# High and low weight words side by side in one buffer, read by TensorE with a step of two words

## The chip, the cores and the metric

The kernel runs on one core of a Trainium2 chip, in one launch. The metric is the device time of that core in microseconds (us). The engines are named as in the profile: PE is TensorE's matmul, PEld its weight load, DVE is VectorE, ACT ScalarE, POOL GpSimd and SP SyncE, which issues the transfers.

## The reference

Two layers of one block and then two layers of another, on 512 tokens of width 1024. Cut to the matrix products that matter here:

```python
# first block, twice
h = x @ w_in[l]                                  # 1024 -> 10k columns
proj   = einsum('bsnc,ncd->bsnd', branches, w_o_branch[l])
merged = sum(sigmoid(merge + b_gate) * proj, axis=2)
x      = layer_norm(alpha * x + merged @ w_out[l])
# second block, twice; in its first layer the 256 context tokens go through too
zx, zc = hx @ w_in[i], hc @ w_in[i]
x, ctx = x + ga1 * (mx @ w_out[i]), ctx + cga1 * (mc @ w_out[i])
x   = x   + ga2 * swiglu(fx, w_gate_up[i], w_down[i])
ctx = ctx + cga2 * swiglu(fc, w_gate_up[i], w_down[i])
```

Everything is float32. A recurrence (RWKV), two attentions, a convolution and a Fourier mix stand between these products; their own matrix products do not use the buffers that are changed.

## The kernel before

**Weights as a stream of chunks.** All weights are laid out in HBM as 414 chunks of 128 partitions by 1024 words; a chunk is eight 128x128 tiles side by side. The class `Stream` (from L92) takes them through a ring of three buffers (`send`, L112). Most chunks, 376 of them, are used at more than one pass of precision: such a chunk is split into a high part of type float32r and a low part, the remainder. ACT makes the high part by a copy with conversion (`hi`, L123), POOL the low part by a subtraction (`lo`, L131). There are two slots for highs and two for lows (`PARTS = 2`). `hi` of a chunk may start when the split chunk two before it has been left by PE, which PE says with a semaphore on the first matmul of the next chunk; `lo` waits for `hi`, and a new transfer into the ring waits for `lo`.

**Products from three passes.** Activations too are held as a high and a low tensor of float32r. For each 128x128 tile of weights PE runs three matmuls: high weights by high activations (L155 or L163), high weights by low activations (L158 or L166), low weights by high activations (L723, L1717, L2140, L2369, L167 and others). In `three` the three passes stand directly one after another for each tile; in the other form the two passes with high weights run over the whole chunk first, and the passes with low weights follow, so that they have more time to be made. The weights are the stationary operand, and PE loads them anew for every matmul, a load of 128 columns. The moving operand is the activation: 512 tokens, or the 256 context tokens in the first layer of the second block.

**What sets the order.** Each stage is a block in which every engine has its own instruction list, written out by hand, with semaphores between them; the lists of PE, ACT and POOL call `stream.hi`, `stream.lo` and the matmul helpers at fixed places. In the last stages of layer 1 (output projection and the two down projections, class `Project`) a chunk is used by `three` and by 512 columns only, and its low part has to be there when its first tile begins.

**One other reader.** Before the feed forward of each layer, and at the opening of the last layer, PE runs ten matmuls on a high part alone, as both operands, while it waits for the norm (L2205). Nothing reads what they write.

The functions below name the parts only as `stream.high(n)` and `stream.low(n)`, which come from the two fields `highs` and `lows` of `Stream`.

Of the kernel before, what the change touches and what calls it, by code (L numbers as in the profile page):

```python
# [17 lines left out]
F32R = mybir.dt.float32r  # L18
# [4 lines left out]
P = 128  # L23
# [17 lines left out]
RING = 3  # L41
PARTS = 2
CW = 1024
# [131 lines left out]
def build(nc, A):  # L175
    with ExitStack() as ctx:
        def sb(name, shape, dt=F32):
            return ctx.enter_context(nc.sbuf_tensor(name, shape, dt))

        pools = [[nc.alloc_semaphore(f"stage{p}_{i}") for i in range(47)] for p in range(3)]  # L180
        arrived = [nc.alloc_semaphore(f"chunk_arrived{i}") for i in range(RING)]
        used = nc.alloc_semaphore("chunks_used")
        hi_made, lo_made = nc.alloc_semaphore("high_made"), nc.alloc_semaphore("low_made")
        loaded = nc.alloc_semaphore("loaded")
        stored = nc.alloc_semaphore("stored")
        constants = nc.alloc_semaphore("second_constants")
        PS = ctx.enter_context(nc.psum_tensor("ps", [P, 8, 512], F32))
        turn = [0]

        def stage():  # L190

            turn[0] += 1
            return Names(pools[turn[0] % 3]), pools[(turn[0] + 1) % 3]

        WR = (sb("ring", [P, RING, CW]), sb("highs", [P, PARTS, CW], F32R), sb("lows", [P, PARTS, CW], F32R),
              arrived, used, hi_made, lo_made)
        mods = sb("mods", [P, LAYERS, 96])

        XH, XL = sb("x_high", [P, DK, T], F32R)[:, :, :], sb("x_low", [P, DK, T], F32R)[:, :, :]
        BR = sb("BR", [P, NB * WT, T])  # L200

        def weights(n):
            if n < SECOND:
                return A["w1"][n // NCHUNK1, n % NCHUNK1, :, :]
            return A["w2"][n - SECOND, :, :]

        split = [NCHUNK1 * layer + n for layer in range(LAYERS) for n in SPLIT1] + SPLIT2
        stream = Stream(WR, weights, split)
        with ExitStack() as one:
            merged = first(nc, one, A, PS, XH, XL, BR, stream, mods, stage, loaded)  # L210
        with ExitStack() as two:
            second(nc, two, A, PS, XH, XL, BR, stream, mods, stage, constants, stored, merged)
# [2888 lines left out]
```

## Time and profile before

| | us |
|---|---|
| median of 2 runs | 3352.69 (3351.68 to 3353.70) |
| the profiled execution | 3352.91 |
| its span in the trace | 3351.1 |
| PE busy in the span | 3206.5 (96%) |
| PEld busy | 2516.6 (75%) |
| POOL, DVE, ACT busy | 1485.4, 1508.9, 1183.9 |
| mean granted TensorE clock | 0.989 of full speed |

The profiled execution is 0.2 us above the median and its span 1.8 us shorter than its time. "Busy" is time in which at least one instruction of the engine is in flight, so that matmuls and loads which overlap are not counted twice in a total, while the mean duration of one is longer than the pace at which they follow one another.

### The profile page before, as it was taken

To read this page: it belongs to the slowest core of one execution; us is meant where nothing else is said; L and a number is where in the kernel's file an instruction comes from. 1 tells how busy PE (TensorE), PEld (TensorE's weight loads), DVE (VectorE), ACT (ScalarE), POOL (GpSimd) and SP (SyncE) were. 2 spreads that over 40 slices of the span, in tenths; PEclk is the share of its full clock that TensorE was granted. 3 is DMA by queue.
4 is the path that set the end of the run, shared out by engine and by line. 5 is a ranking of instruction groups with operands and counts; after the bars stand their busy time and mean duration, and the time that the engine had idled before them with its cause. 6 is when DMAs were issued, how large, how long until landed. Compare 5 with 4: busy or idle time off the path is not lost. (4 is left out here: it accounts for less than half of the span.)

```text
span 3351.1 us, 51795 instructions
## 1 busy us (share of the span) xinstructions
PE 3206.5 (96%) x21120; PEld 2516.6 (75%) x21120; DVE 1508.9 (45%) x2374; ACT 1183.9 (35%) x1940; POOL 1485.4 (44%) x820
## 2 busy tenths in 40 slices
PE   8899999999999999999998989999999998999999
PEld 6784786888668747868876756788888875678787
DVE  7633374999575333949996235300100022520000
ACT  6224433422353434252225445322122243532221
POOL 4421553444353235545442276344234434745454
PEclk9999999999999999999999999999999999999999
DMA  3011132555220111235543200121122211023232
GB/s 130 8 34 57 57 101 76 208 201 191 78 63 4 46 63 64 94 114 196 206 151 109 66 26 27 51 64 63 57 70 63 63 61 51 16 80 101 92 97 94
DMA packets 77611, 284.18 MB, mean 85 GB/s; under 512 B 8736, under 2 KB 8736, under 8 KB 76864
## 3 DMA queue, kind: packets, MB, share of 16 engines
q1 hardware_dynamic: 77376, 280.88, 25.2%
q8 instruction: 168, 2.75, 0.3%
q14 instruction: 67, 0.55, 0.1%
HBM read 278.75 MB, written 2.10 MB: 84 GB/s over the span
## 5 line engine op out<-in xcount | busy, mean ns | idle before, releaser
L131 POOL TENSOR_TENSOR lows<-ring,highs 128x1024 fp32r<-128x1024 f32 x376 | 941.4, 2505 | 1542.5 <-ACT highs L123 1508.3
L155 PE MATMUL ps<-x_high,highs 128*128 128x512 f32 x2080 | 831.5, 400 | 33.7 <-ACT highs L123 14.9
L158 PE MATMUL ps<-x_low,highs 128*128 128x512 f32 x2080 | 814.3, 391 | 0.0
L123 ACT ACTIVATE highs<-ring 128x1024 fp32r<-128x1024 f32 x376 | 397.0, 1056 | 714.6 <-PE ps L155 375.8
L155 PEld LDWEIGHTS ps<-x_high,highs 128*128 128x128 f32 x2080 | 392.4, 189 | 133.6 <-issue 37.8
L158 PEld LDWEIGHTS ps<-x_low,highs 128*128 128x128 f32 x2080 | 392.8, 189 | 83.8 <-issue 4.8
L1790 DVE CUSTOM_DVE_ANT_0 BR<-BR 128x1024 f32<-128x1024 f32 x144 | 289.4, 2010 | 6.8
L2830 DVE TENSOR_TENSOR hidden_scratch<-ps,hidden_scratch 128x512 f32<-128x512 f32 x44 | 30.4, 691 | 546.5 <-PE ps L2140 538.3
L723 PE MATMUL ps<-x_high,lows 128*128 128x512 f32 x1024 | 252.9, 389 | 0.0
L723 PEld LDWEIGHTS ps<-x_high,lows 128*128 128x128 f32 x1024 | 192.2, 188 | 39.9
L2706 DVE SCALAR_TENSOR_TENSOR BR<-ps,mod,BR 128x512 f32<-128x512 f32 x72 | 47.3, 662 | 364.9 <-PE ps L167 364.9
L163 PE MATMUL ps<-hidden_parts,highs 128*128 128x512 f32 (+1 forms) x528 | 188.0, 356 | 0.0
L167 PE MATMUL ps<-hidden_parts,lows 128*128 128x512 f32 (+1 forms) x528 | 188.0, 356 | 0.0
L166 PE MATMUL ps<-hidden_parts,highs 128*128 128x512 f32 (+1 forms) x528 | 188.0, 356 | 0.0
L471 POOL TENSOR_SCALAR tiles<-tiles 128x768 f32<-128x768 f32 (+1 forms) x80 | 154.8, 1947 | 29.0 <-DVE tiles L498 29.0
L2140 PE MATMUL ps<-x_high,lows 128*128 128x512 f32 x672 | 167.1, 391 | 0.0
L1605 DVE SCALAR_TENSOR_TENSOR ps<-X,par,ps 128x512 f32<-128x512 f32 x232 | 152.9, 741 | 0.0
L2140 PEld LDWEIGHTS ps<-x_high,lows 128*128 128x128 f32 x672 | 123.3, 188 | 24.0
L471 POOL TENSOR_SCALAR X<-X 128x256 f32<-128x256 f32 (+3 forms) x96 | 97.7, 1030 | 67.3 <-DVE X L498 67.2
L492 DVE TENSOR_REDUCE tiles<-ps 128x1 f32<-128x768 f32 (+1 forms) x80 | 67.6, 845 | 109.2 <-PE ps L365 109.0
L166 PEld LDWEIGHTS ps<-hidden_parts,highs 128*128 128x128 f32 x528 | 99.4, 188 | 15.8
L163 PEld LDWEIGHTS ps<-hidden_parts,highs 128*128 128x128 f32 x528 | 99.2, 188 | 16.0
(443 smaller groups left out, 5584.6 us busy)
## 6 DMA issues: line engine op xcount, KB each, us to landing
ring<-in_w SPq DMA_DIRECT2D x414, 512.0 KB, 3.5
BR<-in_ada SPq DMA_DIRECT2D x72, 512.0 KB, 3.5
merging<-in_ada SPq DMA_DIRECT2D x24, 512.0 KB, 3.4
X<-in_xT SPq DMA_DIRECT2D x4, 512.0 KB, 6.5
X<-in_memT SPq DMA_DIRECT2D x2, 1024.0 KB, 5.3
BR<-in_cond SPq DMA_DIRECT2D x4, 512.0 KB, 4.7
out<-BR SPq DMA_DIRECT2D x8, 256.0 KB, 4.5
cst<-in_cst SPq DMA_DIRECT2D x1, 1408.0 KB, 8.0
```

What stands on the lines that cost most here:

```text
L123: nc.scalar.activation(self.high(n), self.chunk(n), ACT.Copy).then_inc(self.hi_made, 1)
L131: nc.gpsimd.tensor_tensor(self.low(n), self.chunk(n), self.high(n).bitcast(F32), ALU.subtract).then_inc(self.lo_made, 1)
L155: mm = nc.tensor.matmul(ps, high, xhigh, start=start, stop=False)
L158: nc.tensor.matmul(ps, high, xlow, start=False, stop=False)
L163: mm = nc.tensor.matmul(ps, high, xhigh, start=start, stop=False)
L166: nc.tensor.matmul(ps, high, xlow, start=False, stop=False)
L167: return nc.tensor.matmul(ps, low, xhigh, start=False, stop=stop)
L471: nc.gpsimd.tensor_scalar(prob(i, u), prob(i, u), stats[:, 3, n:n + 1], None, ALU.mult).then_inc(S("normed"), 1)
L723: mm = nc.tensor.matmul(PS[:, bank, :], tile_of(stream.low(n), k), xh[:, k, :], start=False, stop=(k == DK - 1))
L1605: ins = v.scalar_tensor_tensor(out=ACC[:, c, :] if tap == TAPS - 1 else acc, in0=H0[:, c, tap:tap + T], scalar=w, in1=acc, op0=ALU.mult, o ...
L1790: v.tensor_tensor_reduce(PROD, rows_of(t), CB[:, c, :], 1.0, 0.0, ALU.mult, ALU.add, AD[:, t, c:c + 1]).then_inc(S("ada"), 1)
L2140: mm = nc.tensor.matmul(ps, tile_of(stream.low(n), k), high[:, k, :], start=False, stop=(k == DK - 1))
```

## The change

The two tensors for highs and lows, each of 128 partitions by 2 slots by 1024 words, become one of 128 by 2 by 1024 by 2 words: word 0 of each pair is the high part, word 1 the low part. `highs` and `lows` are now views of it whose neighbouring words lie two words (8 bytes) apart. The size in total, the number of slots, all instructions, their order and all semaphores stay as they are. ACT writes with that step (L123), POOL reads the high part and writes the low part with it (L131), PE loads weights with it, and the matmuls of L2205 read their moving operand with it.

```diff
-        WR = (sb("ring", [P, RING, CW]), sb("highs", [P, PARTS, CW], F32R), sb("lows", [P, PARTS, CW], F32R),
-              arrived, used, hi_made, lo_made)
+        ring, parts = sb("ring", [P, RING, CW]), sb("weight_parts", [P, PARTS, CW, 2], F32R)
+        WR = (ring, parts[:, :, :, 0], parts[:, :, :, 1], arrived, used, hi_made, lo_made)
```

## Rows read from the trace of the kernel before

**Rows 1.** The page: busy time of each engine (share of the span), instructions.
```profile
PE 3206.5 (96%) x21120; PEld 2516.6 (75%) x21120; DVE 1508.9 (45%) x2374; ACT 1183.9 (35%) x1940; POOL 1485.4 (44%) x820
```
**Rows 2.** Busy by stretch, instructions touching highs, then lows (PE, PEld, ACT, POOL).
```profile
0.00:3351.10 3351.10, 1748.99 (x7390) 1320.26 (x7390) 397.00 (x376) 941.43 (x376) 0.99 0.26 85
...
0.00:3351.10 3351.10, 954.76 (x3680) 666.12 (x3680) 941.43 (x376) 0.99 0.26 85
```
**Rows 3.** Groups of PE by shape: out<-moving,weights | busy us, mean ns | idle before.
```profile
L158 PE MATMUL ps<-context_low,highs 128*128 128x256 f32 x416 | 101.9, 283 | 0.0
L155 PE MATMUL ps<-context_high,highs 128*128 128x256 f32 x416 | 101.8, 283 | 0.0
L163 PE MATMUL ps<-hidden_parts,highs 128*128 128x256 f32 x176 | 48.9, 278 | 0.0
L2140 PE MATMUL ps<-context_high,lows 128*128 128x256 f32 x336 | 46.9, 282 | 0.0
L163 PE MATMUL ps<-mixed_parts,highs 128*128 128x256 f32 x64 | 17.7, 277 | 0.0
L2369 PE MATMUL ps<-context_high,lows 128*128 128x256 f32 x80 | 11.2, 282 | 0.0
L163 PE MATMUL ps<-context_high,highs 128*128 128x256 f32 x16 | 4.7, 294 | 0.1
...
L723 PE MATMUL ps<-x_high,lows 128*128 128x512 f32 x1024 | 252.9, 389 | 0.0
```
**Rows 4.** Timeline of PE: start us, us from first start to last end, runs.
```profile
1500.08 2.03 PE L1717 MATMUL ps<-branches_high,lows 128*128 128x512 f32 x8
1505.59 1.98 PE L723 MATMUL ps<-x_high,lows 128*128 128x512 f32 x8
...
2256.24 1.12 PE L2140 MATMUL ps<-context_high,lows 128*128 128x256 f32 x8
```
**Rows 5.** Groups of PEld by shape: weight loads of 128, 96 and 64 columns.
```profile
L158 PEld LDWEIGHTS ps<-x_low,highs 128*128 128x128 f32 x2080 | 392.8, 189 | 83.8 <-issue 4.8
...
L1353 PEld LDWEIGHTS ps<-X,ring 128*96 128x96 f32 x96 | 15.5, 163 | 26.1 <-issue 26.1
...
L392 PEld LDWEIGHTS ps<-tiles 128*64 128x64 f32 x832 | 44.7, 137 | 8.9 <-issue 8.9
```
**Rows 6.** Timeline of PE: float32 by 256 columns, moving step one, then two.
```profile
1803.76 1.46 PE L2322 MATMUL ps<-mixed,ring 128*128 128x256 f32 x6
...
1939.99 1.52 PE L2541 MATMUL ps<-ring,tiles 128*128 128x256 f32 x6
```
**Rows 7.** Lines L2322 and L2541: duration ns min/median/max.
```profile
L2322 PE MATMUL ps<-mixed,ring x64: 378/379/380, 1803.5 to 1835.0; 128*128 128x256 f32 x64
...
L2541 PE MATMUL ps<-ring,tiles x80: 386/592/667, 1939.5 to 2826.3; 128*128 128x512 f32 x64, 128*128 128x256 f32 x16
```
**Rows 8.** Waits: who waited for whom, us in total, times, longest.
```profile
POOL lows L131 <- ACT highs L123: 1508.3, 324, 40.1
...
PE ps L155 <- ACT highs L123: 18.5, 11, 7.2
```
**Rows 9.** Lines L131 and L123: duration ns min/median/max.
```profile
L131 POOL TENSOR_TENSOR lows<-ring,highs x376: 2337/2402/3465, 7.2 to 3338.1; 128x1024 fp32r<-128x1024 f32 x188
...
L123 ACT ACTIVATE highs<-ring x376: 1039/1060/1065, 6.1 to 3337.0; 128x1024 fp32r<-128x1024 f32 x188
```
**Rows 10.** Timeline of POOL and ACT in a down projection of layer 1.
```profile
3133.07 2.39 POOL L131 TENSOR_TENSOR lows<-ring,highs 128x1024 fp32r<-128x1024 f32 x1 [3.20 <-ACT highs L123]
...
3131.93 1.06 ACT L123 ACTIVATE highs<-ring 128x1024 fp32r<-128x1024 f32 x1 [4.54 <-PE ps L163]
3137.53 1.06 ACT L123 ACTIVATE highs<-ring 128x1024 fp32r<-128x1024 f32 x1 [4.54 <-PE ps L163]
```
**Rows 11.** Timeline around the warming matmuls of L2205 in layer 1.
```profile
2977.25 3.77 PE L2205 MATMUL ps<-highs 128*128 128x512 f32 x10 [2.53 <-PEq L2718]
...
2982.33 0.47 PE L163 MATMUL ps<-x_high,highs 128*128 128x512 f32 x1 [1.31 <-DVE x_low L2196]
```
## Prediction

> **What bounds the kernel now.** The page comes first: PE is busy for 96% of the span, twice as long as any other engine, so only what PE does or waits for can move the time [rows 1]. The view of busy time by tile says how much of that the change reaches: 7,390 matmuls take their weights from highs and 3,680 from lows, 11,070 of 21,120, with 1,749 and 955 us of PE time [rows 2]. The groups by shape divide these by the width of the moving operand. The 256-column ones are L158 and L155 with 416 each, L163 of hidden_parts with 176, L2140 with 336, L163 of mixed_parts with 64, L2369 with 80 and L163 of the context with 16; each L163 stands for three lines of equal count, L163, L166 and L167 [rows 3]. That is 416+416+336+80+3x(176+64+16) = 2,016, and leaves 9,054 with 512 columns.
>
> The duration of a matmul is no price, since matmuls overlap; the timeline gives the pace. Eight matmuls of L723 in 1.98 us with 0.389 for the last one are (1.98-0.389)/7 = 227 ns each; eight of L1717 with the same end are 234; eight of L2140 with the context, (1.12-0.282)/7 = 120 ns [rows 3, 4]. The pace follows the moving columns: 256 more cost 107 ns. What does a load take beside that? Loads of 128, 96 and 64 columns last 189, 163 and 137 ns [rows 5], so 52 ns for 64 columns, 0.81 ns a column: 128 columns are about 104 ns of reading and 85 ns of fixed delay, an estimate from the slope. Under a 512-column matmul this read has 227-104 = 123 ns of room, under a 256-column one only 120-104 = 16. The 256-column matmuls are thus where a slower load would show first.
>
> **The change part by part.** No instruction, wait or transfer is added, removed or moved; four kinds of instruction get operands whose words lie two apart.
>
> *Weight loads, 11,070.* The trace of before has no weight load with a step. The nearest row is a moving operand with one: L2541, whose 256-column form takes every second word of the ring. Six of these in 1.52 us, ending with one of about 387 ns (the lowest of this line is 386), are (1.52-0.387)/5 = 227 ns each; L2322, the same float32 by 256 columns with neighbouring words, gives (1.46-0.379)/5 = 216 [rows 6, 7]. Step two costs that stream 5%, at 216/256 = 0.84 ns a word, which is about the rate of a load (0.81). I take this 5% for the load: 104 becomes 110 ns, still under 120, and the cost is nothing; the cover is the streaming of the operand of the matmul before it. If the 6 ns came through all the same, it would be 2,016 x 6 = 12 us; under 512 columns, nothing. Gain is excluded, since the moving operand sets the pace. The other end is a load at half its rate; it is the first rival below.
>
> The Trainium skill, "SBUF — State Buffer", under "Door 1: The DMA port swizzle", says that SBUF has lines of 16 bytes and that an engine keeps full rate as long as it finds two or more of its words in each. Step two leaves exactly two, so by that rule the loads and the reads of L2205 cost nothing at all, and the time would be 3354; the trace's 5% for just this step speaks a little against it. The same page also says that each crossing to a new line pays, and the change doubles the crossings, from 32 to 64 for a load; read in that way it is the first rival.
>
> *L2205, 30 matmuls.* Their moving operand is a high part, 512 words of float32r. L723 streams 512 such words in 227 ns; L2541 needs the same 227 ns for 256 words with step two [rows 4, 6]. I take it that the step halves the rate here: 454 ns, 227 more for each, 2.3 us for the ten of a stage. In the trace they end at 2977.25+3.77 = 2981.02 and PE next waits for x_low of DVE until 2982.33, so 1.31 us are free and 1.0 is left over [rows 11]. There are three such stages: 0 to 3 x 2.3 = 7 us; I take 2.
>
> *ACT's 376 copies.* They last 1,039 to 1,065 ns [rows 9]. Their store now steps by two words, which no ACT row shows. Bounds: nothing, and, as for L2205, twice the time, 1.06 us more. PE waits for a high 11 times, 18.5 us in all [rows 8]; 1.06 on each is 12 us. With the 5% of the nearest stepped row it is 0.05 us on each, 1 us with rounding up. I take 1.
>
> *POOL's 376 subtractions.* They last 2,337 to 3,465 ns, in the middle 2,402 [rows 9], now with one read and the store stepped. POOL waits for ACT 1,508 us in all before them [rows 8], so mostly there is room. The tightest place is where `three` needs the low part at once: the 8+2x11 = 30 chunks of the last projections of layer 1. There ACT starts at 3131.93, when PE's first matmul of the chunk before has ended; the low part is ready at 3133.07+2.39 = 3135.46; and the next start of ACT, at 3137.53, says that PE began the chunk about 0.4 earlier, its load 0.2 before that, at 3136.9 [rows 10]. That is 1.4 us of margin. The nearest row for a slower POOL is its own longest, 3,465, or 1.06 us more: covered. Cost nothing. Should POOL or ACT be faster, nothing comes of it beyond PE's waits for highs, at most 18 us [rows 8].
>
> The Trainium skill, "GPSIMD Engine Reference", "Performance pitfalls for Q7 kernels", makes a read half as dear again once step times element size exceeds 8 bytes. The change stands at 8 exactly; no row here tests it, and by its 50%, 1.2 us, the margin would still hold.
>
> **Sum.** Against the profiled execution's 3352.9: loads 0, L2205 +2, ACT +1, POOL 0, which makes 3355.9. That execution lies 0.2 above the median of the runs, so 3356 it is.
>
> **The rivals.**
>
> *Loads at half their rate (slower).* If a load fetches two words at a time and step two wastes one of them, its read takes 2 x 104 = 208 ns. In the 256-column matmuls it then replaces the stream as what sets the pace: 208, or 208+16 = 224 if the present distance stays, against 120. That is 2,016 x 88 to 104 = 177 to 210 us; under 512 columns 224 still fits in 227. Time 3533 to 3566, say 3550. It decides from a load's read of 120 ns on, and reaches 2% (67 us, 33 ns for each) at 153. For it: the halving that I take myself for L2205. Against it: the load is as slow as the stream of L2541, where the step costs 5% and not 100% [rows 5, 6]. Chance 0.19.
>
> *Loads and streams collide more.* The pace at 512 columns is not one number: 227 for L723, 234 for L1717, with the same shapes and other tensors [rows 4], so something beside the count of columns costs up to 7 ns. If it is the load's read meeting the stream's, twice the stretch of memory may bring those 7 ns everywhere: 9,054 x 7 = 63 us, time 3419. Against it: one path of it would have to reach tensors that show none today. Chance 0.05, half of it beyond 2%.
>
> *The makers of the parts fall behind.* ACT at twice its time and POOL at its longest are 2.12 us more against 1.4 of margin: 30 x 0.7 = 21 us, with the 12 us of the waits for highs 3389. Chance 0.04.
>
> *The parts are made faster.* All of PE's waits for highs gone: 3356-18 = 3338. No row points to it. Chance 0.01.
>
> **How the numbers follow.** My forecast has 0.71: 3356, itself from 3343 (run to run and a few of the waits) to 3375 (12 us for the loads, 7 for L2205). The range must hold 8 in 10; with the makers' 3389 and the collision's 3419 it has 0.71+0.04+0.05 = 0.80, so it ends at 3425 and leaves out the first rival; below, 3340. Two per cent, 67 us, is about what a measurement of this kernel tells from no change. Within it: 0.71+0.04+0.01 and half of 0.05, 0.78. Slower: 0.19+0.02 = 0.21. Faster: 0.01.
>
> **What would show it.** Right: L158 and L2140 with 256 columns keep a busy time near 102 and 47 us; loads from highs last between 189 and 195 ns; L2205 paces near 454 ns; POOL and ACT stay within 1.06 us of now. The first rival: loads from highs and lows near 290 ns, and only the 256-column groups longer. The collision: 512-column matmuls at 234 and more wherever the weights come from the new buffer. The makers: waits of PE for L131 in the last projections. The forecast is wrong if a load's read with step two lasts over 120 ns, for then nothing covers it; and far more wrong if it passes 227, for then all 11,070 matmuls pay.

## The result

The changed kernel takes 3391.64 us (3390.48 to 3392.8, two runs) against 3352.69: a ratio of 1.0112 with a 95% interval of 1.0082 to 1.0141, 39 us more. The number lies in the predicted range and within 2%, but 36 us above the forecast of 3356, so most of what there is to learn lies in that gap. Every sign that the prediction listed for being right (the 256-column groups, loads of 189 to 195 ns, L2205 near 454 ns, POOL and ACT within 1.06 us) came true all the same; none of them looks at the 512-column matmuls. The granted clock was 0.989 in this execution and between 0.983 and 0.992 in the others that are compared here; one of the eleven runs of e5_aligned below took 5353 us at a granted clock of 0.554 and is in no ratio.

First, the page of the changed kernel: busy time of each engine, then the groups that hold most of the weight matmuls (busy us, mean ns | idle before, and what ended it).
```profile
PE 3246.7 (96%) x21120; PEld 2578.2 (76%) x21120; DVE 1517.2 (45%) x2374; ACT 1212.6 (36%) x1940; POOL 1495.2 (44%) x820
...
L155 PE MATMUL ps<-x_high,weight_parts 128*128 128x512 f32 x2080 | 842.1, 405 | 31.9 <-ACT weight_parts L123 13.3
L158 PE MATMUL ps<-x_low,weight_parts 128*128 128x512 f32 x2080 | 824.6, 396 | 0.0
...
L155 PEld LDWEIGHTS ps<-x_high,weight_parts 128*128 128x128 f32 x2080 | 406.2, 195 | 129.3 <-issue 34.6
L158 PEld LDWEIGHTS ps<-x_low,weight_parts 128*128 128x128 f32 x2080 | 405.8, 195 | 83.3 <-issue 4.6
...
L723 PE MATMUL ps<-x_high,weight_parts 128*128 128x512 f32 x1024 | 259.5, 394 | 0.0
```
The same groups of the kernel before, as far as they were not shown yet:
```profile
L155 PE MATMUL ps<-x_high,highs 128*128 128x512 f32 x2080 | 831.5, 400 | 33.7 <-ACT highs L123 14.9
L158 PE MATMUL ps<-x_low,highs 128*128 128x512 f32 x2080 | 814.3, 391 | 0.0
```
PE is as full as before, 96%, and busy 40.2 us longer; it does not wait more (31.9 us of idle time before L155 where there were 33.7). A load of 128 columns lasts 195 ns where it lasted 189 [rows 5]. So the time is not in a wait: the matmuls themselves follow each other more slowly, and it is the wide ones. L723 went from 252.9 [rows 3] to 259.5 us.

The groups by shape of the changed kernel, and the two groups of before that they need beside [rows 3], say which ones.
```profile
L163 PE MATMUL ps<-hidden_parts,weight_parts 128*128 128x512 f32 x352 | 138.5, 393 | 0.0
...
L158 PE MATMUL ps<-context_low,weight_parts 128*128 128x256 f32 x416 | 103.1, 284 | 0.0
...
L1717 PE MATMUL ps<-branches_high,weight_parts 128*128 128x512 f32 x256 | 64.4, 393 | 0.0
...
L163 PE MATMUL ps<-hidden_parts,weight_parts 128*128 128x256 f32 x176 | 49.6, 282 | 0.0
...
L2140 PE MATMUL ps<-context_high,weight_parts 128*128 128x256 f32 x336 | 47.6, 284 | 0.0
```
```profile
L163 PE MATMUL ps<-hidden_parts,highs 128*128 128x512 f32 x352 | 139.1, 395 | 0.0
...
L1717 PE MATMUL ps<-branches_high,lows 128*128 128x512 f32 x256 | 65.0, 395 | 0.0
```
The slow-down is not everywhere. L723 takes 6.6 us more over 1,024 matmuls, L158 of x_low 10.3 more over 2,080. But L1717 (branches) and the wide form of L163 (hidden_parts) are no longer than before, 64.4 for 65.0 and 138.5 for 139.1. The 256-column groups cost a little: 101.9 to 103.1, 46.9 to 47.6, 48.9 to 49.6 us [rows 3].

The timeline of the changed kernel's PE (start us, us from first start to last end) gives the pace, as in [rows 4].
```profile
1519.55 2.01 PE L1717 MATMUL ps<-branches_high,weight_parts 128*128 128x512 f32 x8
...
1525.13 2.03 PE L723 MATMUL ps<-x_high,weight_parts 128*128 128x512 f32 x8
...
2266.33 1.13 PE L2140 MATMUL ps<-context_high,weight_parts 128*128 128x256 f32 x8
```
L723 now paces (2.03-0.394)/7 = 234 ns, where it was 227; L1717 (2.01-0.393)/7 = 231, where it was 234; L2140 with the context (1.13-0.284)/7 = 121, where it was 120. The fast stream has joined the slow ones.

To place all of the difference I summed, over the whole trace, the distances from the start of the matmul before to each matmul's own start; a distance is counted with the later of the two. First to last start is 3340.3 us before and 3377.6 after, 37.3 more. Of these, 26.3 are in the 512-column weight matmuls (32.8 more in distances up to 300 ns, which hold hardly any wait, and 6.5 less in longer ones), 7.7 in the 256-column ones, 4.0 in L2205, and 0.7 less in all the rest. Where both matmuls have the same width and take their weights from the changed buffers, the mean distance up to 260 ns is 227.7 before and 233.1 after with x_high, 228.0 and 233.5 with x_low, 229.2 and 233.1 with merged_high; but 230.7 and 231.8 with branches_high, 237.3 and 231.6 with branches_low, 233.1 and 231.2 with hidden_parts.

### The profile page after: what moved, and what is told of

Same layout as the page of the kernel before. It is cut to its first block and busy times, and to the rows that moved or that the text cites. A ratio compares the mean times of both kernels' runs of the same rounds, so it can differ in the third digit from the quotient of the medians.

```text
span 3388.7 us, 51795 instructions
## 1 busy us (share of the span) xinstructions
PE 3246.7 (96%) x21120; PEld 2578.2 (76%) x21120; DVE 1517.2 (45%) x2374; ACT 1212.6 (36%) x1940; POOL 1495.2 (44%) x820
## 5 line engine op out<-in xcount | busy, mean ns | idle before, releaser
L131 POOL TENSOR_TENSOR weight_parts<-ring,weight_parts 128x1024 fp32r<-128x1024 f32 x376 | 950.9, 2530 | 1571.0 <-ACT weight_parts L123 1535.7
L155 PE MATMUL ps<-x_high,weight_parts 128*128 128x512 f32 x2080 | 842.1, 405 | 31.9 <-ACT weight_parts L123 13.3
L158 PE MATMUL ps<-x_low,weight_parts 128*128 128x512 f32 x2080 | 824.6, 396 | 0.0
L123 ACT ACTIVATE weight_parts<-ring 128x1024 fp32r<-128x1024 f32 x376 | 427.0, 1136 | 720.7 <-PE ps L155 380.0
L155 PEld LDWEIGHTS ps<-x_high,weight_parts 128*128 128x128 f32 x2080 | 406.2, 195 | 129.3 <-issue 34.6
L158 PEld LDWEIGHTS ps<-x_low,weight_parts 128*128 128x128 f32 x2080 | 405.8, 195 | 83.3 <-issue 4.6
L1790 DVE CUSTOM_DVE_ANT_0 BR<-BR 128x1024 f32<-128x1024 f32 x144 | 297.6, 2066 | 6.8
L723 PE MATMUL ps<-x_high,weight_parts 128*128 128x512 f32 x1024 | 259.5, 394 | 0.0
L723 PEld LDWEIGHTS ps<-x_high,weight_parts 128*128 128x128 f32 x1024 | 198.1, 193 | 40.9
L167 PE MATMUL ps<-hidden_parts,weight_parts 128*128 128x512 f32 (+1 forms) x528 | 188.3, 357 | 0.0
L166 PE MATMUL ps<-hidden_parts,weight_parts 128*128 128x512 f32 (+1 forms) x528 | 188.2, 356 | 0.0
L163 PE MATMUL ps<-hidden_parts,weight_parts 128*128 128x512 f32 (+1 forms) x528 | 188.0, 356 | 0.0
L2140 PE MATMUL ps<-x_high,weight_parts 128*128 128x512 f32 x672 | 170.4, 394 | 0.0
L2140 PEld LDWEIGHTS ps<-x_high,weight_parts 128*128 128x128 f32 x672 | 127.0, 194 | 23.4
L163 PEld LDWEIGHTS ps<-hidden_parts,weight_parts 128*128 128x128 f32 x528 | 103.0, 195 | 13.0
L167 PEld LDWEIGHTS ps<-hidden_parts,weight_parts 128*128 128x128 f32 x528 | 103.0, 195 | 12.8
```

Source lines behind the costliest of these rows:

```text
L123: nc.scalar.activation(self.high(n), self.chunk(n), ACT.Copy).then_inc(self.hi_made, 1)
L131: nc.gpsimd.tensor_tensor(self.low(n), self.chunk(n), self.high(n).bitcast(F32), ALU.subtract).then_inc(self.lo_made, 1)
L155: mm = nc.tensor.matmul(ps, high, xhigh, start=start, stop=False)
L158: nc.tensor.matmul(ps, high, xlow, start=False, stop=False)
L163: mm = nc.tensor.matmul(ps, high, xhigh, start=start, stop=False)
L166: nc.tensor.matmul(ps, high, xlow, start=False, stop=False)
```

## Experiments

Each ratio below is against runs of the kernel before on the same chip: 3352.87 us (14 runs) for e1_tiles, e2_highs_step, e3_step4 and e4_gap128, 3351.29 (21 runs) for e2b_lows_step, e5_aligned, e6_step_gap128 and e7_gap64, 3350.88 (15 runs) for e8_second_shift128. **Theory A** is that the step is the cause: a load whose words lie two apart slows the stream that runs beside it. **Theory B** is that the common buffer, or where things lie in memory, is.

### One buffer, unit step

In e1_tiles high and low stand side by side in one buffer of the same size, but tile by tile, so that each load still reads 128 neighbouring words (two lines of the edit; the functions that pick a part and a tile follow it).
```
-  WR = (sb("ring", ...), sb("highs", [P, PARTS, CW], F32R), sb("lows", [P, PARTS, CW], F32R),
+  ring, parts = sb("ring", ...), sb("weight_parts", [P, PARTS, DK, 2, P], F32R)
+  WR = (ring, parts[:, :, :, 0, :], parts[:, :, :, 1, :], ...
```


> High and low parts share one buffer, but in runs of 128 words, one tile of weights each, so that every weight load has neighbouring words and only the blocks alternate. Theory A (the load's own step makes it meet the stream of the moving operand more often): the 512-column matmuls by x go back from 233 to about 227 ns, loads last 188 ns again, ACT's copy 1.06 us, time 3353 +- 8. Theory B (what counts is where the parts lie, not the step): the pace stays near 233 for x, time 3375 to 3392. Theory C (the slower copies of ACT, 72 ns, and POOL, 34 ns, disturb PE): as A, this run does not part A from C.

Measured: 3352.57 us, ratio 1.0 (0.9991 to 1.0009). The page of e1_tiles:
```profile
L158 PE MATMUL ps<-x_high,weight_parts 128*128 128x512 f32 x2080 | 832.0, 400 | 33.9 <-ACT weight_parts L123 15.2
L123 ACT ACTIVATE weight_parts<-ring 128x1024 fp32r<-128x1024 f32 x376 | 397.6, 1058 | 714.9 <-PE ps L158 375.2
```
Its L158 is the L155 of the other kernels, with 832.0 us for 831.5. One buffer for both parts costs nothing, so the first half of Theory B falls; the step remains, and the place.

### Only one of the parts stepped

e2_highs_step steps the high parts alone (over the two slots), e2b_lows_step the low parts alone.
```
e2_highs_step
-  sb("highs", [P, PARTS, CW], F32R)       -  return self.highs[:, self.place[n] % PARTS, :]
+  sb("highs", [P, CW, PARTS], F32R)       +  return self.highs[:, :, self.place[n] % PARTS]
e2b_lows_step: the same two lines for lows
```


> Only the highs are read with step two: the highs of the two slots are interleaved word by word, the lows lie as before, the memory is the same. Theory A: matmuls with high weights by x pace at 233, those of L723 with low weights at 227, loads 195 and 188 ns; about two thirds of the 39 us, time 3375 to 3381. Theory B: no such division by the part; both near one value. Theory C: POOL reads a stepped high as in the change and ACT stores one, so both passes would be slow, L723 at 230 to 233.

> Only the low parts step (by two words, over the two slots); the high parts and both sides of x keep unit step. About a third of the weight loads read the lows, all under 512 columns of x_high and its like. Theory A (each stepped load slows the stream beside it by about 6 ns): L723 and the third passes of x go to 233, the others stay at 227.7: about 3,000 loads by 5.5 to 6 ns, 16 to 18 us, and nothing for the fp32r stream of L2205: 3367 to 3372. Rival (one stepped buffer is enough to spoil the pace of all): 3380 to 3390.

Measured: 3379.61 (1.0083, 1.0068 to 1.0098) and 3363.67 (1.0039, 1.0024 to 1.0055). The page of e2_highs_step:
```profile
L123 ACT ACTIVATE highs<-ring 128x1024 fp32r<-128x1024 f32 x376 | 426.6, 1135 | 722.2 <-PE ps L155 380.6
L155 PEld LDWEIGHTS ps<-x_high,highs 128*128 128x128 f32 x2080 | 405.2, 195 | 130.2 <-issue 36.0
...
L723 PE MATMUL ps<-x_high,lows 128*128 128x512 f32 x1024 | 253.8, 390 | 0.0
L723 PEld LDWEIGHTS ps<-x_high,lows 128*128 128x128 f32 x1024 | 192.3, 188 | 41.4
```
And the page of e2b_lows_step:
```profile
L155 PE MATMUL ps<-x_high,highs 128*128 128x512 f32 x2080 | 830.9, 399 | 32.3 <-ACT highs L123 13.1
...
L155 PEld LDWEIGHTS ps<-x_high,highs 128*128 128x128 f32 x2080 | 392.5, 189 | 130.5 <-issue 35.1
L723 PE MATMUL ps<-x_high,lows 128*128 128x512 f32 x1024 | 259.6, 394 | 0.0
L723 PEld LDWEIGHTS ps<-x_high,lows 128*128 128x128 f32 x1024 | 197.8, 193 | 40.5
```
For the streams of x the cost goes with the stepped load. With stepped highs L155's loads last 195 ns, and L723, which loads the lows, keeps 188 ns and 253.8 us; with stepped lows it is the other way round, 193 ns and 259.6 us. That also answers the third theory of e1_tiles, that the slower copies of ACT disturb PE: ACT's copy lasts 1,135 ns with stepped highs, as in the change, and L723 keeps its time. The two add up: 26.7 and 12.4 us are 39.1, and the whole change costs 39.0. e2b_lows_step missed its range by 3 us from below: of the 3,008 wide matmuls with low weights only 2,144 have x_high and 128 merged_high; 2,272 by 5.5 ns are 12.5 us. The narrow matmuls of hidden_parts do not divide by the part: their mean distance is 114.4 ns before, 119.1 with stepped highs, 119.9 with stepped lows though only a third of their loads step, and 120.1 with both. Why is open.

### Twice the step

e3_step4 lets both slots and both parts alternate word by word, so that each operand steps by four words (against the changed kernel).
```
+  ring, parts = sb("ring", ...), sb("weight_parts", [P, CW, PARTS, 2], F32R)
+  WR = (ring, parts[:, :, :, 0], parts[:, :, :, 1], ...
+  return self.highs[:, :, self.place[n] % PARTS]      (lows alike)
```


> High and low of both slots are interleaved, so that loads, copies and subtractions step by four words, 16 bytes, in the same 16 KB. Theory A (a load reads twice the stretch of memory again): the reads of a load take 4 x the stretch of before; if each 16 bytes costs the load what it costs the moving stream in the trace, 227/128 = 1.77 ns, the load's read is 128 x 1.77 = 227 ns, the 512-column pace 235 to 250 and the 256-column pace about 227 to 240 instead of 120, time 3352 + 9054 x 0.01 to 0.02 + 2016 x 0.11 = 3660 to 3760. Theory B: no slower than the change, 3392. L2205's ten matmuls slow to about 900 ns each, 3 x 4.5 us more, partly seen.

Measured: 3732.78 us, ratio 1.1133 (1.1116 to 1.1149), within the range. The page of e3_step4 and two rows of its PE timeline:
```profile
PE 3538.4 (95%) x21120; PEld 3203.3 (86%) x21120; DVE 1575.2 (42%) x2374; ACT 1560.9 (42%) x1940; POOL 1684.2 (45%) x820
...
L123 ACT ACTIVATE weight_parts<-ring 128x1024 fp32r<-128x1024 f32 x376 | 783.0, 2084 | 768.0 <-PE ps L155 381.9
L155 PE MATMUL ps<-x_high,weight_parts 128*128 128x512 f32 x2080 | 866.0, 416 | 61.5 <-ACT weight_parts L123 41.3
...
L158 PEld LDWEIGHTS ps<-x_low,weight_parts 128*128 128x128 f32 x2080 | 647.4, 311 | 5.9
```
```profile
2481.63 2.16 PE L2140 MATMUL ps<-x_high,weight_parts 128*128 128x512 f32 x8
2483.63 1.92 PE L2140 MATMUL ps<-context_high,weight_parts 128*128 128x256 f32 x8
```
Now the load is slow: 311 ns, 122 more than the 189 of before. Added to the 104 of reading that the prediction estimated, that is 226 ns for one read. In these rows the context paces (1.92-0.397)/7 = 218 ns where it was 120, and x_high (2.16-0.398)/7 = 252 where it was 227. By the sum of distances the 2,016 narrow matmuls take 200.8 us more, 100 ns each. This is the first rival of the prediction, within its price (177 to 210 us), one step further than it was feared: what happens to a load whose read outlasts the stream beside it. It also shows that the change's 6 ns under 512 columns are of another kind, for there the read, 110 ns by the same estimate, leaves half of the stream's 227 unused.

The rest of the range was met partly by luck. The 9,024 wide weight matmuls take 149 us more, but 132 of these lie in distances over 300 ns (500 of them, 254 before), and PE's waits for ACT, 46.1 us against 18.5, are the smaller part of that; the rest is not placed. And L2205, which by the rule of 1.77 ns for each 16 bytes was to slow to about 900 ns, took 464. So the rule fits the load (226 for 227 ns) and not the moving operand, and one fit does not show it.

### The step, or the place

e4_gap128 is the kernel before with 128 bytes put between the weights and everything behind them.
```
+  sb("gap", [P, 32])
   mods = sb("mods", [P, LAYERS, 96])
```


> The kernel before with 128 unused bytes between the lows and what follows, so that x, the branches, the hidden and mixed parts all lie 128 bytes further from the weights (merged parts keep their place). Theory B (the pace of 227 or 233 is set by where operands lie, modulo some hundred bytes): x, now 227, goes to about 233 and costs some 6000 x 6 ns = 36 us, the branches go from 233 to 227; time 3375 to 3390. Theory A alone (only the step counts) has no place for it: paces as before, 3353 +- 8.

e7_gap64 has half the gap, e6_step_gap128 puts the gap of 128 bytes into the changed kernel.

> The kernel before, with 64 bytes instead of 128 between the weights and everything behind them. If the pace goes by the offset within 256 bytes, x comes to the offset (64 behind the weights) from which the hidden values' branch-like 233 can be interpolated: x between 228 and 234, hidden and mixed at the offset opposite the weights. Theory D says a time between 3352 and 3372, by how many streams fall on the slow pace; if the kernel is indifferent to offsets under 128 bytes it stays at 3352 to 3354.

> The changed kernel with 128 bytes between the weights and everything behind them. Theory D1 (a load that steps by two words puts every stream at 233, wherever the operands stand): x stays at 233.1 to 233.5, merged at 233, time 3390 to 3393. D2 (the step only moved x from a good place to a bad one, and another place is good): x at 227 to 229 again, time 3355 to 3365. D3 (step and bad place add): x at 238 or more, time 3410 to 3430.

Measured: e4_gap128 3366.45 (1.0039, 1.0025 to 1.0054), e7_gap64 3355.79 (1.0013, 1.0004 to 1.0022), e6_step_gap128 3380.92 (1.0089, 1.0075 to 1.0102). The page and the groups by shape of e4_gap128 (its lines after L196 are one higher):
```profile
L155 PEld LDWEIGHTS ps<-x_high,highs 128*128 128x128 f32 x2080 | 394.3, 190 | 137.4 <-issue 32.4
...
L724 PE MATMUL ps<-x_high,lows 128*128 128x512 f32 x1024 | 259.3, 395 | 0.0
...
L163 PE MATMUL ps<-hidden_parts,highs 128*128 128x512 f32 x352 | 136.7, 388 | 0.0
...
L1718 PE MATMUL ps<-branches_high,lows 128*128 128x512 f32 x256 | 63.2, 389 | 0.0
```
And the page of e6_step_gap128:
```profile
L155 PE MATMUL ps<-x_high,weight_parts 128*128 128x512 f32 x2080 | 837.0, 402 | 32.7 <-ACT weight_parts L123 14.0
...
L155 PEld LDWEIGHTS ps<-x_high,weight_parts 128*128 128x128 f32 x2080 | 408.1, 196 | 122.5 <-issue 35.6
...
L724 PE MATMUL ps<-x_high,weight_parts 128*128 128x512 f32 x1024 | 257.6, 393 | 0.0
```
For e4_gap128 the paces are those of Theory B, the time is a miss for both: it lies under B's 3375 to 3390 and over A's 3353 +- 8. The wide matmuls take 20 us more in distances up to 300 ns, for B's price was that of x alone and other streams give some back, and 7 us less in all the rest, 4.7 of them in matmuls that the changed buffers do not feed. e7_gap64 came within its range. Its expectation puts hidden and mixed values "opposite the weights", but 64 bytes bring them from 192 bytes past the weights' offset to that offset itself. Without any step, and with loads of the same 190 ns, 128 bytes make L724 (the L723 of before) as slow as the change does, 259.3 us, and make the branches and hidden values faster, 65.0 to 63.2 and 139.1 to 136.7. The mean distances are, with the step in the last two rows:

| kernel | x_high | branches_high, _low | hidden_parts, 512 | time, us |
|---|---|---|---|---|
| before | 227.7 | 230.7, 237.3 | 233.1 | 3352.7 |
| e4_gap128 | 231.9 | 227.3, 227.9 | 228.9 | 3366.5 |
| e7_gap64 | 229.4 | 231.8, 235.1 | 227.7 | 3355.8 |
| changed | 233.1 | 231.8, 231.6 | 231.2 | 3391.6 |
| e6_step_gap128 | 231.6 | 232.8, 232.8 | 233.3 | 3380.9 |

So the pace of a stream at unit step depends on where its operand lies. Counted within 256 bytes from the offset at which every tile of the weights begins, it is 226.7 to 228.0 ns at 0 (x before, branches in e4_gap128, hidden values in e7_gap64), 228.9 to 229.4 at 64 (merged values, hidden in e4_gap128, x in e7_gap64), 230.7 to 237.3 at 128 (branches before, x in e4_gap128) and 231.8 to 235.1 at 192 (hidden before, branches in e7_gap64). The weights themselves were moved in none of these kernels, so whether it is the distance to them that counts, or the operand's own address, is not parted.

With the step none of these streams is below 231 at either place. e6_step_gap128 lies between the theories that it was to tell apart, nearer to the first (every stream on the slow pace) in its paces; against the 3351.3 us of before on its chip it adds 30 us where the change adds 39, and the two intervals overlap. Place has an effect of its own, but it does not explain the change: x begins at the same address before and after it, so does the weights' buffer, and e1_tiles, which moves the tiles about in that buffer, costs nothing.

### Using the place

e5_aligned moves branches, hidden and mixed values to the offset that the weights and x have; e8_second_shift128 moves hidden and mixed values alone, by 128 bytes.
```
e5_aligned                                e8_second_shift128
-  sb("room_edge", [P, 8])                -  spare = sb("spare", [P, 16])
+  sb("room_edge", [P, 40])               +  spare = sb("spare", [P, 48])
-  spare = sb("spare", [P, 16])
+  spare = sb("spare", [P, 32])
```


> Unit step, as before the change, and x and the weights keep their addresses. 128 bytes more stand ahead of the room of the branches and 64 more ahead of the hidden and mixed values, so that both start at the same offset within 256 bytes as the weights, as x does. Theory D (two paces at unit step, set by where the moving operand stands against the weights): the branches' 768 512-column matmuls go from a mean of 232.9 ns to about 227.6 (4.1 us), the hidden values' 1,056 from 233.1 to 228 to 229 (4.3 to 5.4 us), the mixed values' 384 from 233.2 to 228 to 229 (1.6 to 2.0 us), all else unchanged: 10.0 to 11.5 us less, 3341 to 3343. Rival (the paces of 233 belong to those streams for another reason, and the shift by 128 bytes earlier helped them by chance): 3352 to 3353, paces unchanged.

> The kernel before, with 128 bytes more ahead of the hidden and mixed values alone; weights, x, branches and merged values keep their addresses. That puts hidden and mixed 64 bytes past the weights' offset within 256 bytes, where e4_gap128 read 228.9 and 229.4 ns for their 512-column matmuls (233.1 and 233.2 before) and 113.3 ns for the 256-column ones of hidden (114.4 before). No stage fed by the branches changes, so nothing is given to the merging stage, in which VectorE is busy 98% of the time. Placement theory: 1,056 by 4.2 ns, 384 by 3.8 ns and some 700 by about 1 ns are 4.4 + 1.5 + 0.7 = 6.6 us less: a ratio of 0.998. Rival (what PE gains in these stages it waits for later, as with the branches in e5_aligned): the paces fall and the ratio stays within 0.001 of 1.

Measured: 3356.68 us, ratio 1.0014 (1.0005 to 1.0023), and 3350.68 us, ratio 0.9995 (0.9986 to 1.0004). The first is a miss: its paces are those of the theory, and it is 5 us slower than the kernel before, clear of its interval, where the theory had 10 to 11.5 us less and its rival no change. The second has the outcome of its rival, lower paces and a ratio of 1 within 0.001. The groups by shape of e5_aligned:
```profile
L163 PE MATMUL ps<-hidden_parts,highs 128*128 128x512 f32 x352 | 137.5, 391 | 0.0
...
L1717 PE MATMUL ps<-branches_high,lows 128*128 128x512 f32 x256 | 63.2, 389 | 0.0
...
L163 PE MATMUL ps<-hidden_parts,highs 128*128 128x256 f32 x176 | 49.6, 282 | 0.0
```
Its busy time in 40 us of the merging stage (PE, PEld, DVE, ACT, POOL), and PE's waits between 740 and 870 us:
```profile
760.00:800.00 40.00, 36.89 (x162) 29.94 (x161) 39.12 (x45) 12.07 (x15) 18.44 (x7) 1.00 0.60 217
```
```profile
PE ps L155 <- ACT highs L123: 3.1, 2, 1.6
PE ps L155 <- DVE merged_low L1762: 2.1, 1, 2.1
```
The paces fell as foreseen: branches to 226.7 ns, hidden to 227.6, mixed to 227.4. The distances up to 300 ns in the 512-column matmuls sum to 15.1 us less than before. But the longer ones sum to 16.7 us more, and the 256-column ones to 3.2 more: hidden_parts with 256 columns went from 114.4 to 119.5 ns, so the place that is good for the wide form is bad for the narrow one, which I had left out.

Of the longer distances one part can be placed. In the merging stages DVE is busy 39.12 of 40 us, before and now, and PE waits for merged_low from DVE (2.1 us between 740 and 870 us, and 0.2 before). An engine that is full and keeps its pace would take back what PE gained and no more; but between the same matmuls these two stages are 2.3 and 3.6 us longer than before (from 598.6 and 1488.7 us of the trace of before). DVE itself worked longer. Its reductions of L1790, before and in e5_aligned:
```profile
L1790 DVE CUSTOM_DVE_ANT_0 BR<-BR 128x1024 f32<-128x1024 f32 x144 | 289.4, 2010 | 6.8
L1790 DVE CUSTOM_DVE_ANT_0 BR<-merging,BR 128x1024 f32<-128x1024 f32 x48 | 94.1, 1960 | 6.7 <-ACT BR L1751 4.7
```
```profile
L1790 DVE CUSTOM_DVE_ANT_0 BR<-BR 128x1024 f32<-128x1024 f32 x144 | 292.4, 2030 | 6.8
L1790 DVE CUSTOM_DVE_ANT_0 BR<-merging,BR 128x1024 f32<-128x1024 f32 x48 | 97.8, 2039 | 8.0 <-ACT BR L1751 6.0
```
They sum to 383.5 us before and 390.2 here, 3.0 and 3.7 more in the two stages. A mean hides two kinds: most last about 1.2 us, but 79 of 192 before, and 81 here, last more than 1.5, mostly 3.3, and every one of these overlaps a subtraction of POOL. e8_second_shift128, whose branches were left alone, has 387.9, so this sum also moves without the branches; one trace of each does not say whether e5_aligned's share comes from the new place or from the timing.

e8_second_shift128 was profiled in the slowest of its eleven runs (3354.28). It was 6.7 us behind the profiled execution of before by 1783 us, 3.7 at 2076 us, where the first matmul with a moved operand starts, and 1.2 at the last start. In these traces the move thus gained some 2.5 us of the 6.6 foreseen; its 256-column matmuls cost 2.2 us where 0.7 were to be saved (117.9 ns for hidden_parts, not 113.3). In time it does not differ from the kernel before by more than the measurement can tell.

## Why the prediction was right and where it was wrong

**PE as the only bound, no new waits: right.** PE's wait for highs went from 18.5 us [rows 8] to 17.9, and POOL's margin held. The view of waits of the changed kernel:
```profile
PE ps L155 <- ACT weight_parts L123: 17.9, 8, 7.4
...
PE ps L163 <- DVE x_low L2196: 5.0, 7, 1.7
```

**The weight loads, 11,070 at no cost: wrong, and this is the step that carried the forecast.** The load itself was sized right: 110 ns of reading for 104, and the load went from 189 to 195. What failed is the sentence "the cover is the streaming of the operand of the matmul before it", with "under 512 columns, nothing". It takes load and stream for two readers that do not disturb each other as long as the shorter one fits. Under 512 columns they cost 26.3 us instead of nothing, under 256 columns 7.7 us (3.8 ns each, where the prediction allowed up to 6), 34.0 us in all, which is nearly the whole miss of 36. That a stepped load under a stream costs this, e1_tiles, e2_highs_step and e2b_lows_step show for x; what the two share is not shown.

**The collision: the rival that happened, mis-sized.** It named the right clue, L723 at 227 and L1717 at 234 with the same shapes [rows 4], and the right sign, "512-column matmuls at 234 and more wherever the weights come from the new buffer". Its 63 us took 7 ns for all 9,054 (30 of them are those of L2205). Some 2,200 of them, with branches, hidden and mixed values, stood at 231 to 237 already and did not go up as a whole; the 6,432 with x, by 5.4 ns, make 35 us, and the others give 2 back (32.8). And its chance of 0.05 rested on "one path of it would have to reach tensors that show none today", an argument that e4_gap128 refutes: 128 bytes make x slow without any step. Two paces for one shape said that something beside the columns already moved the pace; that should have raised this rival well over the halved load.

**The halved load: did not happen at step two** (195 ns, not 290). At step four the load lasts 311 ns and the rival's price comes true.

**L2205: right in the number, by luck.** The 454 ns rest on L2541 taking 227 ns for 256 words with step two, as long as L723 takes for 512. But L2541 works on plain float32, which takes 216 ns for 256 words at unit step [rows 6]; its step costs 5% and shows no halving. No row of before gave a price for a stepped float32r stream. Lines L2205 and L163 in the changed kernel's timeline:
```profile
3008.94 4.87 PE L2205 MATMUL ps<-weight_parts 128*128 128x512 f32 x10 [2.63 <-PEq L2718]
3014.03 0.48 PE L163 MATMUL ps<-x_high,weight_parts 128*128 128x512 f32 x1 [0.22 <-DVE x_low L2196]
```
The median distance of these matmuls is 454 ns. The ten took 1.1 us longer than in [rows 11] and not 2.3, since 12 of the 30 distances, 5 of them in this stage, had already been 426 or 427 ns before. They lie where the granted clock was at its lower level of 1.2 GHz (0.50). In this stage PE had idled for 2.53 us and run four of the ten before it fell. The trace of before in that stretch (the granted clock is the third number from the end):
```profile
2978.30:2981.00 2.70, 2.70 (x7) 1.62 (x5) 1.11 (x2) 1.87 (x3) 0.00 (x0) 0.50 0.49 182
```
With the step the distances behind each stage's first are 453 to 455 ns at 0.50 and 453 to 464 at the full clock, and with a step of four 461 to 467 at either. So the stepped stream is not slowed by the lower clock here, and a second doubling of the step hardly adds to it. The wait for x_low behind the ten fell from 1.31 to 0.22. Over all, L2205 took 4.0 us more and the wait 3.7 less (8.7 to 5.0): a net of 0.3, where 2 was taken.

**ACT and POOL: right in the sum, small in size.** Lines L123 and L131 of the changed kernel (minimum, median, maximum in ns):
```profile
L123 ACT ACTIVATE weight_parts<-ring x376: 1104/1132/1172, 6.3 to 3374.8; 128x1024 fp32r<-128x1024 f32 x188
...
L131 POOL TENSOR_TENSOR weight_parts<-ring,weight_parts x376: 2371/2436/3447, 7.5 to 3376.0; 128x1024 fp32r<-128x1024 f32 x188
```
The copy takes 72 ns more, 7% for the 5% taken, the subtraction 34 more, against [rows 9]. Neither shows in PE's waits.

**What a measurement tells: wrong.** The prediction took 2%, 67 us, for about what can be told from no change. The change's 1.1% is clear of its interval, and with 14 or 21 runs of before the experiments have intervals of 0.1 to 0.2% to either side.

**The two rules of the Trainium skill.** The Trainium skill, "SBUF — State Buffer", "Door 1: The DMA port swizzle", gives full rate for two or more words in each 16-byte line. For the length of a load that is nearly so (189 to 195 at two words to a line, 311 at one), but the load is not the cost: its rule would have made it 3354, and it was 3392. For the float32r stream of L2205 it does not hold, 454 ns for 227, and 464 at one word to a line. The Trainium skill, "GPSIMD Engine Reference", "Performance pitfalls for Q7 kernels", puts its limit above 8 bytes; at 8 bytes the subtraction was 1.4% longer, at the 16 bytes of e3_step4 its mean went from 2,505 to 3,035 ns, 21%, where the page has half again for a read.

## What to carry to other kernels

An operation that fits under another one is not thereby free: ask whether both read the same memory, and take two paces of one shape in the trace of before as a price that the change may spread. Keep the words of stationary weights next to each other; here a step of two cost 5 to 6 ns for each wide matmul that had been on the fast pace, and a step of four, where the load outlasts a narrow stream, a hundred. A gain in pace is worth something only in stages where no other engine is full, so price it stage by stage. Compare operands of the same type before one row's price is taken for another's.

## What was not expected of the hardware

At unit step 512 columns stream in 227 to 237 ns, by where the moving operand lies: 128 bytes moved x_high from 227.7 to 231.9 and branches_low from 237.3 to 227.9. The offset is no full account: hidden_parts with 256 columns took 113.3 ns in e4_gap128 and 117.9 in e8_second_shift128, with weights and hidden values at the same addresses in both. What makes the paces, and by what a stepped load slows a stream, no run here settles. ACT's copy is slowed far more by the second doubling of the step than by the first: 1,060, 1,132 and 2,077 ns at one, two and four words.
